# In the delta rule's inverse, DVE makes each level's factor from the updated matrix; GpSimd's masked products are removed

## The reference

```python
m = jnp.eye(CHUNK) + jnp.where(strict, jnp.einsum('bhcid,bhcjd->bhcij', kb, k) * decay, 0.0)
rhs = jnp.concatenate([v * beta[..., None], kb * jnp.exp(gc)[..., None]], axis=-1)
sol = lax.linalg.triangular_solve(m, rhs, left_side=True, lower=True, unit_diagonal=True)
```

## Time and profile before

| | |
|---|---|
| median of 3 runs (lowest, highest) | 2565.92 us (2564.57, 2569.61) |
| profiled execution, its own time | 2568.53 us |
| its span, instructions | 2566.8 us, 31156 |
| busy: PE, PEld, DVE, ACT, POOL | 79%, 42%, 30%, 20%, 7% of the span |
| chain that ended last, by engine | PE 54%, DMA 24%, DVE 9%, ACT 3%, POOL 0% |
| the loop of the delta rule | levels 1 to 6 of eight heads, one head a turn, from about 1739 to 1960 us |

### The profile page before, as it was taken

The page is one execution under the profiler, slowest core; times in us unless marked ns, Lnnn a source line. Parts: engine busy times, 40 slices in busy tenths (PEclk is TensorE's granted clock), DMA queues, the critical chain, the costliest instruction groups (busy, mean ns, idle before and its releaser), DMA issues.

```text
span 2566.8 us, 31156 instructions
## 1 busy us (share of the span) xinstructions
PE 2026.7 (79%) x12656; PEld 1071.9 (42%) x12656; DVE 779.4 (30%) x1454; ACT 514.3 (20%) x1049; POOL 191.0 (7%) x230
## 2 busy tenths in 40 slices
PE   5899769987799588888888899949997955656655
PEld 1344554434444432323232566627786831212211
DVE  1011453337730310000010577756765120000001
ACT  1223331112210201010000333244442010000000
POOL 0000000012200000000000400004442000000000
PEclk8899889989999799999999999979998977878887
DMA  9701302160041169898989331110001239999996
GB/s 362 274 9 66 131 0 99 66 240 23 1 164 66 67 262 430 341 432 346 431 340 426 139 131 74 66 66 2 2 2 58 93 162 433 432 431 431 429 433 255
DMA packets 57497, 527.07 MB, mean 205 GB/s; under 512 B 2848, under 2 KB 4128, under 8 KB 43040
## 3 DMA queue, kind: packets, MB, share of 16 engines
q1 hardware_dynamic: 55760, 522.55, 49.1%
q10 hardware_dynamic: 1616, 2.76, 0.3%
HBM read 524.26 MB, written 1.05 MB: 205 GB/s over the span
## 4 chain that ended last, share of the span: by engine, by line
PE 54%; DMA 24%; DVE 9%; issue 4%; ACT 3%; SPq 3%; DVEq 1%; PEldq 0%; POOL 0%; POOLq 0%; PEld 0%; ACTq 0%
DMA ring<-in_moe_w 23%; PE bank L432 21%; PE bank L883 11%; PE bank L812 7%; SPq L283 2%; PE bank L868 2%; DVE ring L1581 2%; PE bank L536 2%; PE bank L619 1%; PE bank L642 1%; DVE x L1943 1%; DMA ring<-in_ab_w 1%; PE bank L405 1%; PE bank L929 1%; PE bank L823 1%
## 5 line engine op out<-in xcount | busy, mean ns | idle before, releaser
L432 PE MATMUL bank<-hT,ring 128*128 128x512 f32 (+1 forms) x1504 | 550.9, 524 | 11.4 <-ACT hT L1006 7.2
L883 PE MATMUL bank<-ring,xgs 128*32 128x512 f32 x3072 | 390.8, 666 | 140.4 <-DMA ring<-in_moe_w 132.0
L432 PEld LDWEIGHTS bank<-hT,ring 128*128 128x128 f32 x1504 | 283.8, 191 | 257.3 <-issue 240.1
L883 PE MATMUL bank<-ring,hT 128*32 128x512 f32 x1536 | 209.0, 701 | 95.3 <-DMA ring<-in_moe_w 95.2
L883 PEld LDWEIGHTS bank<-ring,xgs 128*32 128x32 f32 x3072 | 110.6, 121 | 409.1 <-issue 300.4
L1770 DVE TENSOR_TENSOR hT<-sils,bank 128x512 f32<-128x512 f32 x24 | 15.8, 685 | 601.7 <-PEq L911 601.7
L883 PEld LDWEIGHTS bank<-ring,hT 128*32 128x32 f32 x1536 | 57.3, 126 | 241.5 <-issue 191.7
L1776 DVE SCALAR_TENSOR_TENSOR x<-bank,modT,x 128x256 f32<-128x256 f32 x96 | 42.5, 480 | 320.5 <-PE bank L929 320.5
L1435 DVE SCALAR_TENSOR_TENSOR x<-gluR,cols,x 128x256 f32<-128x256 f32 x240 | 116.0, 483 | 15.9 <-issue 0.4
L1244 ACT ACTIVATE sils<-bank 128x512 f32<-128x512 f32 x24 | 13.5, 596 | 331.4 <-PEq L904 331.3
L385 PE MATMUL bank<-ring,act_c 128*32 128x512 f32 x384 | 56.1, 743 | 26.3 <-DMA ring<-in_mod_w 24.5
(11 more groups left out here) (440 smaller groups left out, 2473.6 us busy)
## 6 DMA issues: line engine op xcount, KB each, us to landing
ring<-in_moe_w SPq DMA_DIRECT2D x96, 4096.0 KB, 21.8
ring<-in_mod_w SPq DMA_DIRECT2D x48, 1024.0 KB, 14.2
ring<-in_cd_w SPq DMA_DIRECT2D x6, 4096.0 KB, 17.9
ring<-in_ab_w SPq DMA_DIRECT2D x5, 4096.0 KB, 21.8
ring<-in_ab_wo SPq DMA_DIRECT2D x2, 4096.0 KB, 18.4
ring<-in_cd_wo SPq DMA_DIRECT2D x2, 4096.0 KB, 12.4
x<-in_xT SPq DMA_DIRECT2D x1, 2048.0 KB, 10.2
ring<-in_ab_w SPq DMA_DIRECT2D x1, 2048.0 KB, 15.7
```

What stands on the lines that cost most here:

```text
L432: last = mm(ps[p["no"] % 4][:, p["c0"]:T], w[:, k, :], hT[:, k, p["c0"]:T], start=(k == 0), stop=(k == KD - 1))
L883: last = mm(ps[banks + s][32 * j:32 * j + 32, :], lhs[s][:, 4 * kh + k, 32 * j:32 * j + 32], w[:, j, k, :], start=(kh == 0 and k == 0), st ...
```

## The change

DVE's level writes F first, drains, and makes the next H by one product of F and pmask. POOL's before_level is gone, and its semaphore with it. values() waits for the F of level 1. hmask is now needed for the first level alone.

```diff
-            hmask = sb("hmask", [P, 6, 64], I32, st)
+            hmask = sb("hmask", [P, 1, 64], I32, st)
...
+                    def wide(mask):
+                        return mask.unsqueeze(1).unsqueeze(1).broadcast_to([P, 2, NT, 64])
+
                     dve.wait_ge(sg("gdn_P"), 6 * p + l)
-                    dve.wait_ge(sg("gdn_Hp"), 5 * p + l)
-                    for mask, to, name in ((hmask, Hb[(l + 1) % 3], "gdn_H"), (fmask, Fb[p % 2], "gdn_F")):
-                        V.copy_predicated(to, mask[:, l, :].unsqueeze(1).unsqueeze(1).broadcast_to([P, 2, NT, 64]), P4).then_inc(sg(name), 1)
+                    dve.wait_ge(sg("gdn_F"), 6 * p + l)
+                    V.copy_predicated(Fb[p % 2], wide(fmask[:, l, :]), P4).then_inc(sg("gdn_F"), 1)
+                    dve.drain()
+                    V.tensor_tensor(Hb[(l + 1) % 3], Fb[p % 2], wide(pmask[:, l - 1, :]), ALU.mult).then_inc(sg("gdn_H"), 1)
...
-                    G.tensor_tensor(m, m, to, ALU.mult)
-                    pool.drain()
-                    G.tensor_copy(hmask[:, l, :], m)
-                    pool.drain()
+                    if l == 0:
+                        G.tensor_tensor(m, m, to, ALU.mult)
+                        pool.drain()
+                        G.tensor_copy(hmask[:, 0, :], m)
+                        pool.drain()
...
-                def before_level(p, l):
-
-                    if not 0 <= p < KD:
-                        return
-                    pool.wait_ge(sg("gdn_F"), 6 * p + l)
-                    G.tensor_tensor(Hb[(l + 1) % 3], Fb[p % 2], pmask[:, l - 1, :].unsqueeze(1).unsqueeze(1).broadcast_to([P, 2, NT, 64]),
-                                    ALU.mult).then_inc(sg("gdn_Hp"), 1)
-
                 def values(p, d):
 
                     if not 0 <= p < KD:
                         return
                     if d == 1 and p >= 2:
                         pool.wait_ge(sg("gdn_rhs"), 3 * (p - 1))
+                    pool.wait_ge(sg("gdn_F"), 6 * p + 2)
...
                     p, n = it, it + 1
-                    before_level(p, 1)
-                    before_level(p, 2)
                     values(p, 1)
-                    before_level(p, 3)
                     values(p, 0)
                     masked_decay(n)
-                    before_level(p, 4)
-                    before_level(p, 5)
                     near_blocks(p)
                     decayed_queries(n)
```

## The result

The changed kernel takes 2602.34 us (median of 4 runs, 2597.79 to 2605.08), the kernel before 2565.31; ratio 1.0139, interval 1.0121 to 1.0157: **37 us slower**. The forecast was slower, 2581, with a range to 2600. The direction and the hand-over were right, the size was not, and the time lies outside the range.

The account below looks back on a forecast made before the run. PE was taken to nearly bound the loop, busy 27.2 of 29 us. Five steady turns (8.4), the first turn (2.2), the second (2.1) and the last (2.9) sum to +15.6 on 2565.9: 2581 us, range 2574 to 2600.

Parts of the forecast that it names:

- the hand-over: After the F copy, drain and product make H 0.77 later; PE pays +0.61 at level 2, +0.38 at 3, 0 at 4.
- L1550 lost its stall: At level 1, L1550 is no longer held by POOL's L2142, which gives back 0.25 us of DVE's queue.
- POOL's near_blocks took the turn behind the product: After level 5, near_blocks starts at 1817.48, behind the new DVE product (1817.39 to 1818.08), and takes the next turn.
- level 5 to level 1: From level 5 to the next turn's level 1, DVE still sets the pace; H and R come +0.69 us later.
- turn 0: In the first turn levels 2, 3, 4 pay nearly all of 0.77, while L1550's larger stall goes: 2.2 us.
- DVE wins both ties: At levels 1 and 2 DVE's product gets the SBUF port before POOL, no loss; chance 0.49.
- A: POOL wins the port at level 1 (+9.6) or 2 (+8.4): one lost about 2591, chance 0.20; both 2599, 0.14.
- The sign that was to tell the ties apart: Mean of DVE's new product: 0.69 no tie lost, 0.93 the one at level 1 lost, 1.14 both.
- D: PE's new idle time, 1.7 us a turn, lowers the clock: one slow stretch a turn 2590, two 2599; chance 0.04.
- B: Not slower: POOL gets the port before the level-5 product, first_level's copies take 0.7 each; 2569 us, chance 0.09.
- C: Faster: removed POOL products had held PE through the end of DVE's queue before level 1; 2558 us, chance 0.04.

Follow-up runs that it names:

- e8: The changed kernel with one POOL drain behind masked_decay's wait and one behind that of values(), nothing reordered; 2586.11 us, ratio 1.0063 to the kernel before.
- e5: The changed kernel with useless PE products before the R of level 2 (3) and level 3 (5); 2597.88 us, ratio 1.0122 to the kernel before.
- e1: The kernel before with DVE's two masked copies swapped, F first, then H, POOL's products kept; 2578.93 us, ratio 1.0056.
- e4: The kernel before, H still copied first, but DVE instead of POOL makes the product preparing the next H, right behind F; 2584.15 us, ratio 1.0079.

## Why the prediction was wrong

**The account of the 33.6 us in the loop.** e8 against before: 236.3-218.3 = 18.0, the change itself. e5 against e8: 245.7-236.3 = 9.4, the lost ties (seven at level 2 by 1.11, two at level 1 by 0.89, together 9.6). After against e5: 251.9-245.7 = 6.2, the clock. That the three add up is arithmetic, since each kernel is compared with the next. What the runs add is the name of each: the 9.4 agree with the 9.6 read from the products' durations, and the 6.2 are the steps of 7.6 and turn 0, which went when PE's wait was filled.

**Right: the hand-over.** The forecast's steps were +0.61 at level 2, +0.38 at level 3, nothing at level 4. The steps of e8 are 4.94 for 4.31, 5.39 for 5.00, 6.12 for 6.12. The drain and the product cost 0.09 to 0.10 and 0.69 (forecast 0.08 and 0.69), and e1 showed the mechanism with the order alone. L1550 lost its stall (0.68 for 0.93), and POOL's near_blocks took the turn behind the product.

**A little too small: level 5 to level 1.** The forecast had +0.69; measured 0.79 in step 1-2 and 0.09 in step 5-1, 0.88. first_level ended some 0.2 later than worked out. More is in turn 0, with the first_level before it: it grew by 4.2 where the forecast had 2.2. Its step 5-1 is 11.19 for 9.40, and the table of stretches gives a granted clock of 0.51 from 1766 to 1770, where the kernel before has 0.73 from 1764 to 1768. So the 18.0 hold some clock as well; no run separates it. The forecast's sum up to the last level 5, 15.0, compares with 18.0; that is inside the forecast's own range, which ended 5 us above its sum. As a ratio, e8's 1.0063 (1.0049 to 1.0077) holds the forecast's 15.6 us, 1.0061.

**Wrong: "DVE wins both ties".** This is the step that failed, a term put at nothing: measured 9.4 us. I saw the two ties and priced one lost turn at 1.2 (measured 1.11 and 0.89), but gave all of A, one tie lost or both, 0.34 and no loss 0.49. At level 2 POOL came some 0.01 before DVE in every turn that had the tie, and won every time. The starts could be worked out to some hundredths of a us, and the outcome turned on 0.01. Level 1 came out as forecast, but for the first two turns. In such a case the likeliest case should not have been the one without loss: it needed both coins to fall well. The sign that was to tell the ties apart would have misled, too: the products' mean is 0.930, which the forecast read as "the one at level 1 lost"; it was seven times level 2 and twice level 1.

**Wrong: the clock as a case apart.** D was given 0.04 and added to nothing; measured 6.2 us. But A feeds it: a lost tie makes R wait 1.66 at once (0.57 in e8), and it is behind that wait that the clock fell; in e8 it is 1.00 from 1773 to 1975. By the forecast's own prices the tie at level 2 and one slow stretch a turn are 2598 to 2599, and the range ended at 2600. B did not come: all eight level-5 products take 0.69, so POOL never got the port ahead of them. Neither did C: the step 5-1 is no shorter in turns 0 to 5, 9.51 to 11.31 for 9.40 to 9.46.

## What to carry to other kernels

Before moving an operation ahead of a signal, list who waits for the signal and, as e4 taught, who stands behind the operation in its own queue; an idle engine's work that is off the path is worth nothing when removed. Where two engines ask for SBUF reads within some hundredths of a microsecond of each other in every turn of a loop, don't guess the winner: put the ends of the range at all lost, and in the kernel move one of them on purpose, if only by a drain. A new wait on PE is to be priced with the clock that may follow it.

## What the runs showed of the hardware that I had not expected

- Two starts 0.01 us apart in the profile decide 1.1 us, and decide it the same way in turn after turn: POOL 0.01 to 0.02 ahead (after, e5), product 1.80 at level 2 and 1.58 at level 1; DVE 0.05 to 0.08 ahead, product 0.69 and POOL's 1.54 (after, level 1) or 1.75 (e8, level 2). That fits the rule of the Trainium skill (SBUF — State Buffer, "Who interferes with whom") that who issues first holds the shared pair for the whole instruction.
- One wait of 1.66 us in front of R was followed by a stretch at 0.57 to 0.59 of the clock in turns 1, 3 and 6 and not in 2, 4 and 5; with useless products in the wait no stretch behind level 2 ran slow. In e4 it fell in turns 2 and 6 behind shorter waits, 1.22 before R and 0.65 before state_out, and with the same two waits it stayed at 1.00 in turns 3 to 5. What tells the turns apart stays open.
- Filling PE's waits with useless products made the loop 6 us shorter (251.9 to 245.7); in the whole time that is too little to tell (ratios 1.0139 and 1.0122, with overlapping intervals).
